# The spread product of the second mixer contracts over all 128 rows instead of 24

## The reference, cut to what matters

```python
cs = jnp.cumsum(dt_c * a, axis=2)                       # per position and head, in chunks of 128
decay = jnp.exp(jnp.where(causal, cs_l - cs_s, -inf))   # within a chunk
y_diag = (cb * decay) @ x_dt
y_off = einsum('bclgn,bcgrpn,bclgr->bclgrp', c_c, prev, jnp.exp(cs))
y = y_diag + y_off + xs * d_skip
```

## Time and profile before

| | |
|---|---|
| median of 3 executions | 1731.17 us (1730.94 to 1731.2) |
| span of the profiled execution | 1728.1 us |
| part of the median outside the profiled span | 3.1 us |
| PE busy / DVE / ACT / POOL in the span | 1704.1 / 1148.4 / 1098.1 / 1230.8 us |
| the 16 spread products (L1383) | first at 436.2, last at 613.0 us |
| steps with head pairs | 436.2 to 463, 492 to 519, 547 to 574, 599.5 to 617 us |

### The profile page before, as it was taken

How to read it: one execution, slowest core, us unless ns; L and a number is a source line. 1 busy time by engine, 2 the same in 40 slices (tenths; PEclk the granted TensorE clock), 3 DMA queues, 4 the chain that set the end, 5 groups by cost and what they waited for, 6 DMA issues and landing times.

```text
span 1728.1 us, 27117 instructions
## 1 busy us (share of the span) xinstructions
PE 1704.1 (99%) x9708; PEld 1031.6 (60%) x9708; DVE 1148.4 (66%) x1965; ACT 1098.1 (64%) x1566; POOL 1230.8 (71%) x1776
## 2 busy tenths in 40 slices
PE   7999999999999999999999999999999999999999
PEld 4556666655555556666665666666656665566665
DVE  6986777228888865777328858775247886677720
ACT  7887666446877756666445776665555665866632
POOL 7867777877556648777877657778766553777785
PEclk9999999999999999999999999999999999999999
DMA  7334444546233325544554124445433332444453
GB/s 273 113 98 134 147 147 142 157 151 177 74 98 100 96 86 169 150 147 148 151 152 132 38 74 140 147 148 153 150 122 102 96 99 75 134 149 147 148 157 119
DMA packets 65614, 226.53 MB, mean 131 GB/s; under 512 B 8149, under 2 KB 9045, under 8 KB 65109
## 3 DMA queue, kind: packets, MB, share of 16 engines
q1 hardware_dynamic: 64236, 221.89, 41.0%
q10 hardware_dynamic: 1245, 2.92, 0.6%
HBM read 222.48 MB, written 2.10 MB: 130 GB/s over the span
## 4 chain that ended last, share of the span: by engine, by line
PE 83%; ACT 7%; DVE 6%; issue 3%; POOL 1%; DMA 0%; SPq 0%; DVEq 0%; ACTq 0%; POOLq 0%
PE psum L310 26%; PE psum L320 25%; PE psum L352 13%; PE psum L356 12%; DVE psum L1655 1%; ACT w_big L251 1%; PE psum L2329 1%; PE psum L1884 1%; PE psum L2365 1%; ACT psum L1499 1%; ACT L1534 1%; PE psum L1929 1%; DVE arena L1700 1%; ACT psum L1534 1%; PE psum L2346 0%
## 5 line engine op out<-in xcount | busy, mean ns | idle before, releaser
L281 POOL TENSOR_TENSOR w_rest<-w_panel,w_big 128x256 bf16<-128x256 f32 x1660 | 1168.4, 741 | 419.9 <-ACT w_big L251 419.0
L310 PE MATMUL psum<-x_big,w_big 128*128 128x512 f32 x2248 | 653.0, 423 | 7.3 <-ACT x_big L402 6.5
L320 PE MATMUL psum<-x_rest,w_rest 128*128 128x512 bf16 x2248 | 555.9, 382 | 1.9 <-DVE x_rest L505 1.9
L251 ACT ACTIVATE w_big<-w_panel 128x1024 fp32r<-128x1024 f32 (+1 forms) x414 | 417.0, 1032 | 171.1 <-PE psum L356 95.4
L310 PEld LDWEIGHTS psum<-x_big,w_big 128*128 128x128 f32 x2248 | 415.7, 189 | 127.2 <-issue 18.2
L320 PEld LDWEIGHTS psum<-x_rest,w_rest 128*128 128x128 bf16 x2248 | 188.2, 98 | 281.5 <-issue 101.8
L738 DVE SCALAR_TENSOR_TENSOR psum<-ffn_raw,params,psum 128x512 f32<-128x512 f32 x352 | 264.4, 751 | 7.2 <-ACT psum L692 1.0
L730 DVE TENSOR_TENSOR ffn_raw<-psum,rstd 128x512 f32<-128x512 f32 x176 | 121.2, 691 | 129.0 <-PE psum L320 119.9
L692 ACT ACTIVATE psum<-ffn_raw,params 128x512 f32<-128x512 f32 x176 | 137.4, 782 | 101.2 <-DVE ffn_raw L730 101.0
L352 PE MATMUL psum<-g_big,w_big 128*128 128x512 f32 x704 | 199.6, 423 | 0.0
L572 DVE SCALAR_TENSOR_TENSOR x_resid<-psum,x_resid 128x512 f32<-128x512 f32 x64 | 43.8, 688 | 224.2 <-PE psum L356 216.3
(11 more groups left out here) (281 smaller groups left out, 1654.8 us busy)
## 6 DMA issues: line engine op xcount, KB each, us to landing
w_panel<-in_up SPq DMA_DIRECT2D x176, 512.0 KB, 3.5
w_panel<-in_dn SPq DMA_DIRECT2D x64, 448.0 KB, 3.2
w_panel<-in_ssd_in SPq DMA_DIRECT2D x41, 512.0 KB, 3.5
w_panel<-in_dn SPq DMA_DIRECT2D x32, 512.0 KB, 3.5
w_panel<-in_hgrn_in SPq DMA_DIRECT2D x32, 512.0 KB, 3.5
w_panel<-in_lru_in SPq DMA_DIRECT2D x18, 512.0 KB, 3.6
w_panel<-in_ssd_out SPq DMA_DIRECT2D x16, 512.0 KB, 3.5
w_panel<-in_swa_in SPq DMA_DIRECT2D x12, 512.0 KB, 3.5
```

The source lines that it names most:

```text
L251: act.activation(k.w1[:, slot, 0:words], k.w[:, slot, 0:words], ACT.Copy, scale=(SHIFT - 1) / SHIFT).then_inc(k.s("panel_big"), 1)
L281: rest = pool.tensor_tensor(k.w2[:, slot, a], k.w[:, slot, a], k.w1[:, slot, a].bitcast(F32), ALU.subtract)
L310: pe.matmul(out, k.w1[:, slot, q * m:(q + 1) * m], k.x1[:, q, :], start=q == 0, stop=False)
L320: mm = pe.matmul(out, k.w2[:, slot, q * m:(q + 1) * m], k.x2[:, q, :], start=False, stop=q == DT - 1)
```

## The change

The product contracts over all 128 rows of the two tables instead of over the 24 that count. For that the table of pairs is loaded in all 128 rows, zeros included: the transfer is 512 KB in the place of 96 KB, each row of 1 KB read once for each of four groups.

```diff
-        self.right, self.pairs = k.y2[:, 0:SSD_T:SSD_TG, :], k.y2[0:SSD_ROWS, 1:SSD_T:SSD_TG, :]
+        self.right, self.pairs = k.y2[:, 0:SSD_T:SSD_TG, :], k.y2[:, 1:SSD_T:SSD_TG, :]
...
-        pe.matmul(k.ps[:, 7, 0:384], b.pick_pair(g, r), b.right[0:SSD_ROWS, g, P:],
+        pe.matmul(k.ps[:, 7, 0:384], b.pick_pair(g, r), b.right[:, g, P:],
                   start=True, stop=True).then_inc(k.s("ssd_cs_spread"), 1)
...
-    for rows, lo, to in ((slice(SSD_ROWS, P), 0, b.right), (slice(0, SSD_ROWS), S // 2, b.pairs)):
+    for rows, lo, to in ((slice(SSD_ROWS, P), 0, b.right), (slice(0, P), S // 2, b.pairs)):
         words = k.dram["ssd_tables"][rows, SSD_LEFT + lo:SSD_LEFT + lo + S // 2]
```

## The result

The changed kernel takes 1733.06 us (median of 20 executions, 1732.46 to 1735.13) beside 1730.57 us for the kernel before in the same comparison (1730.16 to 1731.2): ratio 1.0016, 95% interval 1.0011 to 1.0022. That is 2.5 us slower. It is under the 0.2% that the prediction calls a difference, but outside what this measurement leaves to chance, and about eight times the +0.3 us forecast. It also lies inside the range of 1729.4 to 1733.1 us, by 0.04 us.

A forecast was written before the change was run, and what follows sets the result against it. It took ACT's work to bound the first three groups and a PE-DVE loop the last. Terms: -0.3 us product, +0.6 transfer, +0.3 on the profile's 1728.1, giving 1728.4, or 1731.5 us as median; range 1729.4 to 1733.1.

The forecast's parts named there:

- the product: Each of 16 spread products on PE loses its 0.32 us row-change cost; stretch 1.86 to 1.54 us, 5.1 us in all.
- Rival C: Spread keeps its 0.48 us on PE; only the transfer's +0.6 us is left, giving 1731.8 us; chance 0.03.
- the rule cited for a cost of nothing: Trainium skill on PE weight loads: 32 rows take as long as 128, so the saving would be 0 for all 16.
- where the saving goes: First three groups: 3.8 us leave PE's queue but return as waiting, since ACT's step stays 6.86 us; nothing reaches the end.
- Rival A: PE bounds every group, so all its saved time counts: 4.2 to 5.1 us faster, 1726.1 to 1727.0 us; chance 0.07.
- the return in both waits: PE's waits at L1390 and L1409, at each group's end, grow by 1.3 us a group together.
- the last group: Its first spread is on the chain, -0.3 us; the other three, 0.96 us, go into PE's wait for DVE.
- the chain of the transfer: Larger table delays the panel issued at 401, then ACT's rounding, table load, SiLU and PE's tile at 412.89; +0.6 us.
- The slack: Between the SiLU's end at 412.69 and PE's tile at 412.89: 0.2 us of panel delay absorbed before PE is late.
- X: Lateness of the landing of the panel issued at 401: bounded by 0 and 2.4 us, taken as 0.8.
- Rival B: Larger table holds up the DMA engines all panels share, X over 4.0 us: over 3.5 us slower; chance 0.05.
- ACT waits for several panels in a row after 405: One of the stated signs that the prediction is wrong: ACT held up by several successive panel landings after 405.

The follow-up runs named there:

- the two runs without table loads: SiLU in the second mixer replaced by a copy: kernel before (24 rows) 1727.86 us; changed product with its 512 KB table loaded late (128 rows) 1725.58 us.
- the run with large pieces: Kernel before plus an added 384 KB load in 48 pieces of 8 KB behind ACT's tables: 1730.77 us beside 1729.6, ratio 1.0006.
- The table alone: Kernel before with only the pairs transfer grown to 128 rows (512 KB), spread product still 24 rows: 1732.68 us beside 1730.14, ratio 1.0015.

## Why the prediction was wrong

**Right: the product.** 0.32 us a spread, 1.86 to 1.54 us. Rival C fell, and with it the rule cited for a cost of nothing: the weight load of 24 rows does take as long as that of 128 (91 and 98 ns), but between products of 128 rows the short product costs more (0.48 us from start to start, beside 0.16).

**Right: where the saving goes.** ACT's step stays, PE's dip of 0.66 us at 450 is given back by 467, in all three groups, and the two runs without table loads show that ACT is what hides it: take the table loads away, and 2.1 of the 3.8 us arrive. Rival A needed ACT's step to shrink; it holds only in those two runs. The prediction had the return in both waits. In this trace L1390 takes more of it (1.1 us beside 0.4), and the rest lies in the longer second and third steps; L1409 has the same 0.6.

**Right: the last group.** It gains 0.3 us at the first spread; what the second one saves is given back by 620 in the loop through DVE.

**Right: the chain of the transfer.** The panel issued at 401, L251, the table load, the SiLU and the tile of 412.89 are what the delay went through: the landing is 2.9 us late and the tile 2.9 (415.78 - 412.89), of which 0.1 lay ahead of the stretch. The slack was mis-sized, 0.2 us in place of 0.06.

**Wrong: the size of X.** The step that failed is "I take 0.8, nearer to the low end". X is 2.9 us between the first two profiles (412.56 and 409.65), which is over the bound of 2.4 too; between the means of the two profiles of each kernel (11.4 and 11.0 beside 8.6 and 9.9) it is 2.0, and over all the traces above 1.7, which is under the bound. With 2.9 the prediction's own sum gives -0.3 + 2.7 = +2.4, where these two spans are 2.6 apart.

Two premises failed. The first is that the table is old when the panel comes: it was issued at the mixer's start, but its last packets sat behind the 92-row transfer until 404 and later. The second is the room: a share of busy DMA engines of 0.67 looked like a third of free time. It is an average that hides full engines behind empty ones, and what decides is the rate of the few that lag. There the tail ends at 411.2 in place of 406.8. From 404 to 408 the changed kernel has even less, 0.52 beside 0.63, while its panels wait. The prediction cited the very rule on the number of engines, but used it only for the new transfer, and said that it spoke for neither end; used on the 92 rows, it gives four engines. The landing of 8.6 us for a panel, where 3.5 is usual over the 41 loads of this kind, was the sign in the trace that some engines were behind.

**Luck: the range.** The measured 1733.06 us lies within the stated range by 0.04 us, and that is no merit of the sum. Its upper end counts from 1731.17 us, a median of three executions that in the comparison came out as 1730.57; counted from there it would be 1732.5. The profile of before was of a quicker execution as well. The 3.1 us between median and span come from that: every later execution takes 1.8 us more than its own span (1.75 to 1.96).

Rival B had the mechanism, engines that all panels share being held up; its X of over 4.0 us was not reached.

**Missed: an earlier panel.** "I am wrong if ACT waits for several panels in a row after 405": there are three waits, 4.4 us, but the longest (2.73 us) ends at 404.74, and those after 405 are of 0.26 and 1.45 us. The second profile of before has three as well, 2.9 us in all. The panel rounded at 404.74 makes PE 0.6 to 0.8 us late already at 406, which the later wait then absorbs.

Still open is how much of X is the number of packets and how much their bytes, since the run with large pieces falls between. Nor do the medians close in full. Of the 2.5 and 3.2 us between them, 0.3 and 0.8 go with the executions of a lower granted clock. Those with the full clock are 2.2 and 2.4 us over before. The stretch makes 2.7 and 2.6 us in the two profiles after, 0 and 1.0 in the two of before, which is 2.1 in the mean, less 0.3 in the last group 1.8. The other 0.4 to 0.6 us have no cause shown. In the pair of repeats (spans 2.3 us apart) 0.6 lie ahead of 378, where the kernels do the same, 1.6 in the stretch, and 0.4 behind 620, so differences of this size come and go between executions. The table alone leaves the same: 2.5 us at the full clock, where its trace has 2.5 in the stretch and before 0.5 in the mean.

## What to carry to other kernels

Before a transfer is grown, look at what stands ahead of it in the queues, and divide the row counts: here one transfer of 92 rows left some four engines far behind, and what was added then waited at their rate, not at the stretch's mean. When landings near the change are well above the usual time of the same load (8.6 us beside 3.5), take the high end. A saving on the busiest engine was worth nothing in the groups whose chain runs through ACT; one run with that other engine's load cut tells.

## What the runs showed of the hardware

- Going from products of 128 rows to one of 24 or 64 and back costs PE 0.32 us here, once for the way there and back (stretches of 1.86 and 1.85 us and, with two short products together, 2.00; 1.54 with 128 rows). The Trainium skill's "TensorEngine Tiling (Array Packing)", section "Key Properties", says that changing the tiling mode drains the engine. The loss fits that rule; its size is from the runs, and no run shows that it is a drain.
- With a transfer of 92 rows ahead of them, the panels issued at about 392, 395 and 401 took 10.8, 10.0 and 8.6 us; with it cut into 12 and 80 rows, 8.4, 7.8 and 5.2 us, with more bytes in all.
- Landing times of the same panel in the same kernel differ by 1.3 and 1.8 us between two profiles (8.6 and 9.9, 6.9 and 8.7), and 1 us of it reaches PE. A single profile of before is not enough for a forecast of tenths of a us here.
- A mean granted clock under 1.0 (0.998 or 0.999) shows only in kernels that load the 128-row table right behind the 92-row transfer: in 11 of 41 executions, against 0 of 156 of all the others whose clock is on record.
